# Narrow S5 kernel products, a final norm by rows, S5 scans in two parts and paired first blocks in a two-layer streaming encoder

## The chip, the cores and the metric

The kernel runs on 1 core of one Trainium2 chip. The metric is the time of one launch on the device in microseconds, as the median of several runs; less is better.

## The reference

Two layers over L = 528 positions (16 meta tokens, 512 real ones) of D = 1024 channels. Each layer projects the normalized stream once, feeds three mixers, gates, merges and projects back; a last RMSNorm ends it.

```python
for layer in range(2):
    u = _rmsnorm(h, norm_g[layer])
    (gq, gk, gv, ga, g_gate, s_in, s_gate, aq, ak, av, a_gate, m_gate) = _split_in(u @ w_in[layer])
    y_gla = (_gla_mixer(gq, gk, gv, ga, ...) * silu(g_gate)) @ w_gla_out[layer]
    y_s5  = (_s5_mixer(s_in, ...)            * silu(s_gate)) @ w_s5_out[layer]
    y_att = (_swa_mixer(aq, ak, av, ...)     * silu(a_gate)) @ w_attn_out[layer]
    gates = sigmoid(m_gate).reshape(B, L, 3, D)
    mix = gates[:, :, 0] * y_gla + gates[:, :, 1] * y_s5 + gates[:, :, 2] * y_att
    h = h + mix @ w_out[layer]
return _rmsnorm(h, final_norm_g)[:, 16:]
```

The S5 mixer runs a complex diagonal recurrence with 64 states for each group of 16 channels, then `y = gelu(y)` and `y * sigmoid(y @ w_glu)`.

## The kernel before

Everything lies channel-major: a tensor of 1024 channels is eight tiles (`kt`) of 128 partitions by 528 positions. Every large product is done in blocks of 128 output channels. A block is 24 weight tiles: weights and activations are split into a high and a low part in a rounded float type, and `WH·xh`, `WH·xl` and `WL·xh` are summed over the 8 `kt`, in two halves of 264 columns in layer 0 (48 matmuls) and mostly one of 512 in layer 1 (24).

The blocks of a layer stand in one fixed list, `BLOCKS`: ga, gk (4), gv (8), gq (4), gg (8), aq (8), ak, av; blocks of the merge of GLA (mg0 and wgla by turns, then sin, 8) between the attention steps; then `S5F` (ag, 8, and mg2 and watt by turns, 16) with the S5 steps between them; glu (8), sg (8), mg1 and ws5 by turns (16), wout (8). SyncE loads the raw weights of block n+3 into one of three slots when block n is done (`load_block`); ScalarE copies them to the high part (`hi_part`, L1143), GpSimd subtracts to the low part (`lo_part`, L641). TensorE (`project`, L756; `project_as_made`, L738, where the input comes tile by tile) writes a block into one of two PSUM slots (`RING`), and ScalarE or VectorE `take` it out. Small products go through two further PSUM slots in a fixed order (`AUX`).

S5 matrices: for each of the eight channel tiles j of layer m VectorE makes C·A^k (`cam`) and A^k·B (`mbm`), TensorE transposes them and multiplies them to the local kernel (`toep`, L805, with the skip term, L810), ScalarE evicts them, SyncE spills them to DRAM. All of this is done in layer 0, for m = 0 between gk3 and gq0 (`MATS_0`), for m = 1 between sg6 and wout4 (`MATS_1`).

S5 steps, in the stage of `S5F`: after block i = 3 TensorE computes `step_inputs(0)` (L1071). After block i = 6 + 2j it computes `step_outputs(j)` (L1084, L1086), which wait for `x_state` j, and `step_inputs(j+1)`. VectorE runs `s5_scan(ly, j+1)` after its take of the same block: products with phases from PSUM, the rotation (L1451), a copy of decays (L1943), two scans (L1946), four products and two sums to the state. VectorE's take of a watt block is one reading (L1557) and one add into the mix; an mg2 block it doesn't read.

```python
if i in S5_OUT:
    step_outputs(j)
    if j + 1 < KT:
        step_inputs(j + 1)
```

After the last wout block: squares (ScalarE), sums over channels by TensorE (L781), variance, root, reciprocal (L1499), eight scalings (L2024), 32 transposes (L1126), four copies, four stores.

Of the kernel before, what the change touches and what calls it, by code (L numbers as in the profile page):

```python
# [18 lines left out]
ALU = mybir.AluOpType  # L19
# [77 lines left out]

MATS_0 = [("gk", 3)] + [("gv", j) for j in range(1, 8)] + [("gq", 0)]
MATS_1 = [("sg", 6)] + [("ws5", j) for j in (0, 1, 2, 3, 5)] + [("wout", j) for j in (0, 2, 4)]
# [26 lines left out]
def layer_sums(ly):  # L126
# [16 lines left out]
       + layer_sums(0) + layer_sums(1))  # L143
# [17 lines left out]
def trunk(nc, x, meta_tokens, rel_bias, norm_g, w_in, gla_w_a2, gla_b_a, gla_norm_g, s5_a_re, s5_a_im,  # L161
# [3 lines left out]
    with ctx:  # L165
# [63 lines left out]
        IK = sb("s5_int", [P, DEPTH, PAIRS], I32, at=r)  # L229
        o_tmp = top[0]  # L230
# [50 lines left out]
        def mat_buffers(m, at_bb, at):  # L281
# [10 lines left out]
                toep=sb(f"s5_toep{m}", [P, QUADS, 4, 32], at=at),  # L292
                brep=sb(f"s5_brep{m}", [P, 2, QUADS, 4, 32], at=at),
                ct=[sb(f"s5_c{m}_{i}", [P, 2, QUADS, S5_GROUP], at=a) for i, a in enumerate((at_bb, at))],
                cin=sb(f"s5_c_in{m}", [P, 2, 2, 2, S5_STATE], at=at),
                dsk=sb(f"s5_skip_diag{m}", [P, P], at=at),
                eyes=sb(f"s5_skip_rows{m}", [P, 4, 32], at=at))
# [17 lines left out]
        U = sb("u_full", [P, KT, L], at=[o_ul, o_ul + WIDE])  # L315

# [40 lines left out]
        out_ready, out_stored = sem("out_ready"), [sem(f"out_stored{i}") for i in range(2)]  # L357
        fin_ready = sem("fin_ready")
        dve_step, act_step, pool_step = sem("dve_step"), sem("act_step"), sem("pool_step")

        def aux(ly, name):

            e = AUX_AT[(ly, name)]
            return e % 2, e // 2

        def aux_out(i):
            e = len(AUX) + i
            return e % 2, e // 2
# [59 lines left out]
        def aux_result(engine, ly, name):  # L428

            h, k = aux_out(name) if isinstance(name, int) else aux(ly, name)  # L430
            engine.wait_ge(aux_full[h], k + 1)
            return h

        def spilled(engine, m, j):

            engine.wait_ge(mats_spilled[j % 2], 48 * (4 * m + j // 2) + 48)
# [15 lines left out]
        def _(sp):  # L452
# [57 lines left out]
            def spill_mats(m, j):  # L510
# [10 lines left out]
                sp.dma_start(mat_part(d, "toep"), MB[m]["toep"][:].rearrange("p q t i -> p (q t i)")  # L521
                             ).then_inc(mats_spilled[j % 2], 16)
# [36 lines left out]
            for ly in range(DEPTH):  # L559
                for b in range(NB):  # L560
                    n = ly * NB + b
                    name = BLOCKS[b]
                    if name == _MERGE0[0]:

                        evacuated(sp, ly, ("ak", 0))
                        sp.dma_start(AKD[64:128, 0, :], AKD[0:64, 0, :]).then_inc(akd_loaded, 16)
                        sp.dma_start(AKD[0:64, 1, :], AKD[64:128, 1, :]).then_inc(akd_loaded, 16)
# [37 lines left out]
                    if name == ("sg", 0):  # L605
                        sp.wait_ge(yt_loaded, 256 * ly + 256)
                        sp.dma_start(H[:], HD).then_inc(h_back, 16)
                    if n + SLOTS < DEPTH * NB:
                        load_block(n + SLOTS)
            for t in range(SEQ // P):  # L610
                sp.wait_ge(out_ready, t + 1)
                sp.dma_start(out[0, P * t:P * t + P, :], XIN[:, t % 2, :]).then_inc(out_stored[t % 2], 16)
            sp.wait_ge(out_stored[0], 32)
            sp.wait_ge(out_stored[1], 32)
# [3 lines left out]
        def _(pool):  # L618
# [84 lines left out]
            for ly in range(DEPTH):  # L703
                work = phases(ly)
                for b in range(NB):
                    lo_part(ly * NB + b)
                    if b >= PHASE_FIRST:
# [4 lines left out]
        def _(pe):  # L712
# [30 lines left out]

            def project(ly, b, xh, xl):
# [27 lines left out]
            def norm_sum(k0, name, ly):  # L772

                h = aux_take(ly, name) if name else None
                if h is None:
                    h, k = aux_out(0)
                    pe.wait_ge(aux_free[h], k)
                for kt in range(KT):
                    pe.wait_ge(sq_ready, k0 + kt + 1)
                    for hf, c0, c1 in column_parts(0 if name else N_META):  # L780
# [12 lines left out]
            def step_matrices(m, j):  # L793
# [9 lines left out]
                for q in range(QUADS):  # L803
                    for ri in range(2):
                        last = pe.matmul(AX_[:, 2 * h, P * q:P * q + P],  # L805
                                         MB[m]["brep"][:, ri, q].rearrange("p a b -> p (a b)"),
                                         MB[m]["cam"][:, j % 2, ri, q, 0:4].rearrange("p a b -> p (a b)"),
                                         start=(ri == 0), stop=(ri == 1))
                        if ri == 0:
                            pe.matmul(AX_[:, 2 * h, P * q:P * q + 32],  # L810
                                      MB[m]["eyes"][:].rearrange("p a b -> p (a b)"),
                                      MB[m]["dsk"][:, 32 * q:32 * q + 32],
                                      start=False, stop=False)
                last.then_inc(aux_full[h], 1)

            def mat_turn(ly, b):
# [7 lines left out]
                if k + 1 < KT:  # L824
                    transpose_c(m, k + 1)

# [31 lines left out]
            for ly in range(DEPTH):  # L858
                norm_sum(KT * ly, ("norm", 0), ly)
                project_as_made(ly, ("ga", 0), UH, UL, ulo_ready, KT * ly)  # L860
# [10 lines left out]
                for b in BLOCKS[1:17]:  # L871
# [227 lines left out]
                project_as_made(ly, ("glu", 0), GH, GL, ylo_ready, 32 * ly + 16)  # L1099
                for j in range(1, KT):  # L1100
# [18 lines left out]

            norm_sum(KT * DEPTH, None, 0)  # L1120
            pe.wait_ge(fin_ready, KT)
            for t in range(SEQ // P):
                h, k = aux_out(1 + t)
                pe.wait_ge(aux_free[h], k)
                for kt in range(KT):
                    last = pe.transpose(AX_[:, 2 * h + kt // 4, P * (kt % 4):P * (kt % 4) + P],  # L1126
                                        H[:, kt, N_META + P * t:N_META + P * t + P], ID[:])
                last.then_inc(aux_full[h], 1)
# [3 lines left out]
        def _(act):  # L1132
# [73 lines left out]
            def matrices_out(m, j):  # L1206
# [7 lines left out]
                for p in range(STRIDE):  # L1214
                    rows = slice(32 * p, 32 * p + 32)
                    last = act.activation(
                        MB[m]["toep"][rows, :, STRIDE - 1 - p:STRIDE],
                        AX_[rows, 2 * h].rearrange("p (q t i) -> p q t i", q=QUADS, t=STRIDE)
                        [:, :, 0:p + 1], ACT.Copy)
                last.then_inc(aux_free[h], 1)  # L1220
# [32 lines left out]
            for ly in range(DEPTH + 1):  # L1253

                t0 = N_META if ly == DEPTH else 0
                for kt in range(KT):
# [7 lines left out]
                    act.activation(TA[:, kt % 2, t0:], H[:, kt, t0:], ACT.Square).then_inc(sq_ready, 1)  # L1264
                act.wait_ge(var_ready, ly + 1)
                act.activation(TD[:, 1, t0:], TD[:, 0, t0:], ACT.Sqrt).then_inc(std_ready, 1)
                if ly == DEPTH:
                    break
# [39 lines left out]
                for b in BLOCKS:  # L1308
# [4 lines left out]
                    if kind == "gv" and j % 2 == 0:  # L1313
                        log_sigmoid(j // 2)
                        if j:
                            decay_to_end(j // 2 - 1)
                    if b == ("gq", 0):
# [9 lines left out]
                    if kind == "ws5":  # L1327
                        t0 = first(ly, kind)
                        act.wait_ge(mix_ready, KT * ly + j + 1)
                        act.activation(MXH[:, j, t0:], MIX[:, j, t0:], ACT.Copy).then_inc(mhi_ready, 1)  # L1330
                    mat_turn(ly, b)
# [106 lines left out]


        @block.vector  # L1440
        def _(dve):
# [49 lines left out]
            def inverse_rms(ly, name):  # L1491

                h = aux_result(dve, ly, name)
                t0 = N_META if ly == DEPTH else 0
                dve.tensor_scalar(two(TD[:, 0], t0), halves(aslot(h), t0), 1.0 / D_MODEL, EPS, ALU.mult, ALU.add
# [3 lines left out]
                link(dve.reciprocal(TD[:, 0, t0:], TD[:, 1, t0:]))  # L1499
# [70 lines left out]
            def gla_gates(ly):  # L1570

                for hd in range(GLA_HEADS):
                    h = aux_result(dve, ly, ("gate", hd))
# [484 lines left out]
```

## Time and profile before

| | us |
|---|---|
| median of 3 runs | 1992.9 (1989.21 to 1995.55) |
| profiled execution | 1990.12 |
| its span | 1988.3 |
| TensorE busy (matmul) | 1824.9, 92% of the span |
| VectorE busy | 980.3, 49% |
| ScalarE busy | 713.2, 36% |
| GpSimd busy | 781.4, 39% |

The profile is of one execution. An engine's busy time is a mean over stages with different limits; the chain that ended last is 68% TensorE. Where TensorE waits, a view of waits names the engine and line which released it. A matmul row covers a run of like instructions; numbers in brackets are idle time before the row and who ended it.

### The profile page before, as it was taken

To read this page: it belongs to the slowest core of one execution; us is meant where nothing else is said; L and a number is where in the kernel's file an instruction comes from. 1 tells how busy PE (TensorE), PEld (TensorE's weight loads), DVE (VectorE), ACT (ScalarE), POOL (GpSimd) and SP (SyncE) were. 2 spreads that over 40 slices of the span, in tenths; PEclk is the share of its full clock that TensorE was granted. 3 is DMA by queue.
4 is the path that set the end of the run, shared out by engine and by line. 5 is a ranking of instruction groups with operands and counts; after the bars stand their busy time and mean duration, and the time that the engine had idled before them with its cause. 6 is when DMAs were issued, how large, how long until landed. Compare 5 with 4: busy or idle time off the path is not lost.

```text
span 1988.3 us, 29697 instructions
## 1 busy us (share of the span) xinstructions
PE 1824.9 (92%) x12351; PEld 1636.7 (82%) x12351; DVE 980.3 (49%) x1565; ACT 713.2 (36%) x1271; POOL 781.4 (39%) x475
## 2 busy tenths in 40 slices
PE   6977899999988999879998999999999799899996
PEld 4977898899988999879997987777788688778884
DVE  7988124422428983277663132523333589634223
ACT  3354332444542222233333453333455222223321
POOL 2544565333223333333331586653332323334440
PEclk8988899899998999989999998999999999999998
DMA  8443336222254545524443332532222645443331
GB/s 146 124 148 123 102 86 139 70 75 73 56 129 145 176 139 118 145 69 139 132 129 93 104 96 83 110 107 80 67 72 70 166 167 185 107 133 102 94 94 56
DMA packets 349758, 221.27 MB, mean 111 GB/s; under 512 B 49589, under 2 KB 338537, under 8 KB 347065
## 3 DMA queue, kind: packets, MB, share of 16 engines
q1 hardware_dynamic: 347320, 189.75, 35.8%
q10 hardware_dynamic: 2304, 29.62, 4.0%
q8 instruction: 98, 1.61, 0.3%
q14 instruction: 36, 0.29, 0.0%
HBM read 171.65 MB, written 38.50 MB: 106 GB/s over the span
## 4 chain that ended last, share of the span: by engine, by line
PE 68%; DVE 14%; POOL 5%; DMA 5%; SPq 3%; ACT 2%; issue 2%; ACTq 0%; DVEq 0%; POOLq 0%
PE ring L756 51%; DMA sb_w_raw<-in_w_in 3%; PE ring L738 3%; POOL sb_w_lo L641 2%; PE aux L992 2%; DVE sb_s_mat_prod L1451 2%; PE aux L1084 1%; PE aux L1071 1%; SPq L555 1%; PE aux L805 1%; DVE sb_s_gelu_lo L1451 1%; DVE sb_s_prod L1451 1%; PE aux L1037 1%; PE aux L1013 1%; PE aux L781 1%
## 5 line engine op out<-in xcount | busy, mean ns | idle before, releaser
L641 POOL TENSOR_TENSOR sb_w_lo<-sb_w_raw,sb_w_hi 128x1024 fp32r<-128x1024 f32 x246 | 607.2, 2470 | 1107.0 <-ACT sb_w_hi L1143 1104.7
L1143 ACT ACTIVATE sb_w_hi<-sb_w_raw 128x1024 fp32r<-128x1024 f32 x246 | 259.8, 1057 | 636.3 <-DMA sb_w_raw<-in_w_in 421.4
L756 PE MATMUL ring<-sb_u_hi,sb_w_hi 128*128 128x264 f32 (+1 forms) x2144 | 366.4, 324 | 38.8 <-DVE sb_tmp_dve L1522 28.2
L756 PEld LDWEIGHTS ring<-sb_u_hi,sb_w_hi 128*128 128x128 f32 x2144 | 311.1, 197 | 71.6 <-DVE sb_tmp_dve L1522 29.7
L756 PE MATMUL ring<-sb_u_lo,sb_w_hi 128*128 128x264 f32 (+1 forms) x2144 | 346.9, 313 | 0.0
L756 PE MATMUL ring<-sb_u_hi,sb_w_lo 128*128 128x264 f32 (+1 forms) x2144 | 338.7, 308 | 0.0
L756 PEld LDWEIGHTS ring<-sb_u_lo,sb_w_hi 128*128 128x128 f32 x2144 | 306.6, 193 | 22.3
L756 PEld LDWEIGHTS ring<-sb_u_hi,sb_w_lo 128*128 128x128 f32 x2144 | 298.0, 188 | 21.1
L1175 ACT ACTIVATE sb_tmp_act<-ring 128x528 f32<-128x528 f32 (+1 forms) x112 | 67.5, 603 | 152.1 <-PE ring L756 139.3
L1381 ACT ACTIVATE sb_att_scores<-sb_att_scores,sb_att_neg_max 128x208 f32<-128x208 f32 x128 | 58.5, 458 | 93.9 <-DVE sb_att_neg_max L1741 93.9
L756 PE MATMUL ring<-sb_y_hi,sb_w_hi 128*128 128x264 f32 (+1 forms) x504 | 87.3, 322 | 0.0
L756 PE MATMUL ring<-sb_y_lo,sb_w_hi 128*128 128x264 f32 (+1 forms) x504 | 86.3, 321 | 0.0
L756 PE MATMUL ring<-sb_y_hi,sb_w_lo 128*128 128x264 f32 (+1 forms) x504 | 86.3, 320 | 0.0
L756 PEld LDWEIGHTS ring<-sb_y_lo,sb_w_hi 128*128 128x128 f32 x504 | 73.6, 188 | 7.4
L756 PEld LDWEIGHTS ring<-sb_y_hi,sb_w_lo 128*128 128x128 f32 x504 | 73.5, 188 | 7.4
L756 PEld LDWEIGHTS ring<-sb_y_hi,sb_w_hi 128*128 128x128 f32 x504 | 73.1, 188 | 6.8
L1451 DVE TENSOR_TENSOR sb_y_lo<-sb_o_branch,sb_y_hi 128x528 fp32r<-128x528 f32 (+1 forms) x48 | 50.6, 1071 | 49.3 <-ACT sb_y_hi L1159 48.8
L1557 DVE SCALAR_TENSOR_TENSOR sb_tmp_dve<-sb_tmp_act,ring 128x528 f32<-128x528 f32 (+1 forms) x32 | 22.2, 695 | 105.4 <-PE ring L756 92.1
L1522 DVE SCALAR_TENSOR_TENSOR sb_tmp_dve<-sb_tmp_act,ring 128x528 f32<-128x528 f32 (+1 forms) x32 | 22.2, 695 | 104.1 <-ACT sb_tmp_act L1175 103.8
L1159 ACT ACTIVATE sb_y_hi<-sb_o_branch 128x528 fp32r<-128x528 f32 (+1 forms) x48 | 29.6, 633 | 76.3 <-DVE sb_o_branch L1529 55.1
L1451 DVE TENSOR_TENSOR sb_mix<-sb_mix,sb_tmp_dve 128x528 f32<-128x528 f32 (+1 forms) x32 | 55.2, 1726 | 1.1
L1557 DVE SCALAR_TENSOR_TENSOR sb_mix<-sb_tmp_act,ring 128x528 f32<-128x528 f32 (+1 forms) x16 | 11.1, 696 | 89.4 <-PE ring L756 76.3
(312 smaller groups left out, 2695.8 us busy)
## 6 DMA issues: line engine op xcount, KB each, us to landing
sb_w_raw<-in_w_in SPq DMA_DIRECT2D x166, 512.0 KB, 4.0
sb_s_loaded<-s_matrices ACTq DMA_DIRECT2D x16, 1808.0 KB, 7.3
s_matrices<-sb_s_phase SPq DMA_DIRECT2D x16, 528.0 KB, 3.2
s_matrices<-sb_s_mbt SPq DMA_DIRECT2D x16, 512.0 KB, 2.8
s_matrices<-sb_s_ca SPq DMA_DIRECT2D x16, 512.0 KB, 4.2
sb_w_raw<-in_w_gla_out SPq DMA_DIRECT2D x16, 512.0 KB, 3.9
sb_w_raw<-in_w_attn_out SPq DMA_DIRECT2D x16, 512.0 KB, 4.0
sb_w_raw<-in_s_w_glu SPq DMA_DIRECT2D x16, 512.0 KB, 4.0
```

The costliest lines, as they stand in the source:

```text
L555: sp.dma_start(BM[rows, p], bias_view(REL_ZERO - N_META - P * p - CHUNK * half, CHUNK, N_META)).then_inc(bias_in, 16)
L641: pool.tensor_tensor(WL[:, w], WR[:, w], WH[:, w].bitcast(F32), ALU.subtract).then_inc(lo_ready, 1)
L738: last = pe.matmul(RING[:, 2 * r + hf, 0:c1 - c0], w[:, n % SLOTS, kt, :], moving(b[0], xx[:, kt], c0, c1), start=(term == 0 and kt == 0), ...
L756: last = pe.matmul(RING[:, 2 * r + hf, 0:c1 - c0], w[:, n % SLOTS, kt, :], moving(b[0], xx[:, kt], c0, c1), start=(term == 0 and kt == 0), ...
L992: last = pe.matmul(AX_[:, 2 * h + a, c0:c0 + n], AQ[rows, 2 * i + h2, q0:q0 + P], AKD[rows, i // 2, keys:keys + n], start=True, stop=True)
L1143: act.activation(WH[:, w], WR[:, w], ACT.Copy).then_inc(hi_ready, 1)
L1159: act.activation(YH[:, j, t0:], src[:, t0:], ACT.Copy).then_inc(yhi_ready, 1)
L1175: act.activation(two(TA[:, t % 2], t0), ps, ACT.Tanh, scale=0.5).then_inc(done, 1)
L1381: act.activation(SC[:, u % 2, hd], SC[:, u % 2, hd], ACT.Exp, bias=NMX[:, hd:hd + 1], accum_out=SMM[:, hd:hd + 1])
L1451: return dve.tensor_tensor(o, a, b, op)
L1522: dve.scalar_tensor_tensor(two(td, t0), two(TA[:, t % 2], t0), 1.0, ps, ALU.add, ALU.mult).then_inc(free, 1)
L1557: dve.scalar_tensor_tensor(two(td, t0), two(TA[:, t % 2], t0), 1.0, ps, ALU.add, ALU.mult).then_inc(free, 1)
```

## The change

Eight edits:

- The local S5 kernel is multiplied with weights of 32 columns, eight products into four groups of PSUM partitions and one for the skip term; the copies `eyes` and `brep` and three of four evictions go. The tile is stored with six DMAs for each j in place of three.
- The matrices of m = 1 start one block earlier, their input matrices three blocks earlier, and GpSimd clears their tiles instead of VectorE.
- ScalarE adds the gates' bias instead of VectorE; in layer 1 `log_sigmoid` follows gv 0, 1, 3, 5.
- The blocks (ga0, gk0) and (glu0, glu1) are computed together, tile by tile of their input.
- The duplicate of the attention keys is copied one block earlier.
- `s5_scan` becomes a generator: its second part (scans, products, state) runs one block of `S5F` later, after that block's take.
- A small square root, so that ScalarE's table is loaded, stands ahead of the squares of each norm.
- The final norm: each finished wout tile is transposed to rows while the next block runs; squares and sums are along rows, the scale is applied to [token, channel] tiles.

```diff
-MATS_1 = [("sg", 6)] + ...
+MATS_1 = [("sg", 5)] + ...
...
+            def project_two_as_made(ly, bs, xh, xl, made, base):
+                for b, n in zip(bs, ns):
+                    r, k = ring(ly, b)
+                    if k:
+                        pe.wait_ge(slot_free[r], k)
+                    pe.wait_ge(hi_ready, n + 1)
+                    pe.wait_ge(lo_ready, n + 1)
+                for kt in range(KT):
+                    pe.wait_ge(made, base + kt + 1)
+                    for b, n in zip(bs, ns):
...
-                    for ri in range(2):
-                        last = pe.matmul(AX_[:, 2 * h, P * q:P * q + P],
-                                         MB[m]["brep"][:, ri, q].rearrange("p a b -> p (a b)"),
-                                         MB[m]["cam"][:, j % 2, ri, q, 0:4].rearrange("p a b -> p (a b)"),
...
+                for ri in range(2):
+                    for q in range(QUADS):
+                        pe.matmul(AX_[32 * q:32 * q + 32, 2 * h, 0:P], mbm[:, ri, q, 0],
+                                  cam[:, ri, q, 0:4].rearrange("p a b -> p (a b)"),
+                                  start=(ri == 0), stop=False)
+                pe.matmul(AX_[:, 2 * h, 0:32], ID[:], MB[m]["dsk"][:], start=False, stop=True
...
-                    if name == _MERGE0[0]:
+                    if name == ("av", 0):
...
                 link(dve.tensor_copy(dk[:, :, 1:STEPS],
                                      AB[:, 2, ly, qs].unsqueeze(2).broadcast_to([P, QUADS, STEPS - 1])))
+                yield
                 for ri in range(2):
                     last = dve.tensor_tensor_scan(rr[ri], MM[:, 0], rr[ri], 0.0, ALU.mult, ALU.add)
...
                         for i, f in enumerate(S5F):
                             take(ly, f)
...
                             if i in S5_OUT and S5_OUT[i] + 1 < KT:
-                                s5_scan(ly, S5_OUT[i] + 1)
+                                scan = s5_scan(ly, S5_OUT[i] + 1)
+                            next(scan, None)
...
+            def tokens_out(j):
+                evacuated(pe, DEPTH - 1, ("wout", j))
+                h = aux_take(1, ("fin", j))
+                for t in range(SEQ // P):
+                    last = pe.transpose(AX_[:, 2 * h, P * t:P * t + P],
+                                        H[:, j, N_META + P * t:N_META + P * t + P], ID[:])
...
+            def token_squares(j):
+                h = aux_result(act, 1, ("fin", j))
+                act.activation(FSQ[:, j % 2].rearrange("p t d -> p (t d)"), AX_[:, 2 * h], ACT.Square
...
+            def tokens_in(j):
+                tt(XO[:, :, P * j:P * j + P], AX_[:, 2 * h].rearrange("p (t d) -> p t d", d=P),
+                   FG[:, P * j:P * j + P].unsqueeze(1).broadcast_to([P, 4, P]), ALU.mult).then_inc(aux_free[h], 1)
+                link(dve.reduce_sum(FSS[:, :, j], FSQ[:, j % 2], AX.X))
...
+            link(act.activation(WARM[:, 0:1], ONES[:, 0:1], ACT.Sqrt))
+            token_squares(KT - 1)
...
+            for t in (2, 3):
+                act.activation(XO[:, t], XO[:, t], ACT.Copy, scale=FV[:, 0, t:t + 1]).then_inc(out_ready[1], 1)
...
+            for t in (0, 1):
+                dve.tensor_scalar(XO[:, t], XO[:, t], FV[:, 0, t:t + 1], None, ALU.mult).then_inc(out_ready[0], 1)
```

## Rows read from the trace of the kernel before

**Rows 1.** TensorE's waits over the span: total us, times, longest us.

```profile
PE aux L799 <- DVEq L1919: 28.3, 8, 8.8
PE ring L756 <- DVE sb_tmp_dve L1522: 28.2, 5, 9.2
...
PE ring L738 <- DVE sb_tmp_dve L1522: 11.3, 1, 11.3
...
PE aux L1126 <- DVE sb_residual L2024: 10.3, 1, 10.3
...
PE aux L992 <- DMA sb_att_k<-sb_att_k: 3.1, 1, 3.1
```

**Rows 2.** Windows of the S5 scans, layers 0 and 1: window, length, then busy times.

```profile
637.00:733.00 96.00, 96.00 (x808) 95.93 (x807) 87.02 (x109) 21.23 (x27) 29.49 (x12) 1.00 0.54 180
1599.00:1697.00 98.00, 97.69 (x552) 83.94 (x551) 88.81 (x114) 23.41 (x30) 29.64 (x12) 1.00 0.55 180
```

**Rows 3.** Timeline of VectorE in one turn of that stage: start us, us.

```profile
668.75 2.55 DVE L1451 TENSOR_TENSOR sb_s_prod<-aux,sb_s_loaded 128x528 f32<-128x528 f32 x4 [1.60 <-PE aux L1071]
...
674.49 2.41 DVE L1946 TENSOR_TENSOR_SCAN sb_s_rot<-sb_s_prod,sb_s_rot 128x528 f32<-128x528 f32 x2
...
679.53 1.32 DVE L1451 TENSOR_TENSOR sb_s_state<-sb_s_prod 128x524 f32<-128x524 f32 x2
680.88 0.70 DVE L1557 SCALAR_TENSOR_TENSOR sb_tmp_dve<-sb_tmp_act,ring 128x528 f32<-128x528 f32 x1
681.62 2.01 DVE L1451 TENSOR_TENSOR sb_mix<-sb_mix,sb_tmp_dve 128x528 f32<-128x528 f32 x1
```

**Rows 4.** Timeline of TensorE in the same turn.

```profile
664.85 0.61 PE L1084 MATMUL aux<-sb_s_state,sb_s_loaded 128*128 128x132 f32 x4
...
667.55 2.03 PE L1071 MATMUL aux<-sb_s_steps,sb_s_loaded 128*128 128x132 f32 x16
669.34 2.18 PE L756 MATMUL ring<-sb_y_hi,sb_w_hi 128*128 128x264 f32 x16
...
675.22 2.10 PE L756 MATMUL ring<-sb_u_hi,sb_w_hi 128*128 128x264 f32 x16
...
681.02 0.61 PE L1084 MATMUL aux<-sb_s_state,sb_s_loaded 128*128 128x132 f32 x4
```

**Rows 5.** Timeline of GpSimd in the same turn.

```profile
680.35 2.73 POOL L641 TENSOR_TENSOR sb_w_lo<-sb_w_raw,sb_w_hi 128x1024 fp32r<-128x1024 f32 x1 [7.55 <-ACT sb_w_hi L1143]
```

**Rows 6.** Timeline of VectorE and TensorE around the first scan.

```profile
615.77 4.52 DVE L1946 TENSOR_TENSOR_SCAN sb_s_rot<-sb_s_prod,sb_s_rot 128x528 f32<-128x528 f32 x2
...
625.04 3.57 PE L756 MATMUL ring<-sb_u_hi,sb_w_hi 128*128 128x264 f32 x16 [7.66 <-DVE sb_tmp_dve L1522]
```

**Rows 7.** Timeline of four engines at the start of glu, layer 0.

```profile
769.25 0.78 PE L738 MATMUL ring<-sb_s_gelu_hi,sb_w_hi 128*128 128x264 f32 x2 [3.26 <-DVE sb_s_gelu_lo L1451]
...
770.77 1.99 ACT L1143 ACTIVATE sb_w_hi<-sb_w_raw 128x1024 fp32r<-128x1024 f32 x2
...
771.89 5.36 POOL L641 TENSOR_TENSOR sb_w_lo<-sb_w_raw,sb_w_hi 128x1024 fp32r<-128x1024 f32 x2 [3.36 <-ACT sb_w_hi L1143]
...
778.46 0.71 DVE L1451 TENSOR_TENSOR sb_mix<-sb_mix,sb_tmp_dve 128x528 f32<-128x528 f32 x1
...
784.56 2.09 PE L756 MATMUL ring<-sb_s_gelu_hi,sb_w_hi 128*128 128x264 f32 x16
```

**Rows 8.** Timeline of TensorE at the first block of layer 0.

```profile
35.92 0.78 PE L738 MATMUL ring<-sb_u_hi,sb_w_hi 128*128 128x264 f32 x2 [8.76 <-DVE sb_u_lo L1451]
```

**Rows 9.** VectorE's groups by form, matrices of layer 0: busy us, mean ns.

```profile
L1917 DVE COPY sb_s_brep<-sb_s_mb 128x512 f32<-128x512 f32 x16 | 12.9, 849 | 0.0
```

**Rows 10.** Timeline of the end.

```profile
1958.29 7.59 PE L781 MATMUL aux<-sb_tmp_act,sb_ones 128*128 128x512 f32 x16
...
1979.47 6.05 SPq L612 DMA_DIRECT2D out<-sb_x_tokens  x4
...
1981.26 1.09 PE L1126 MATMUL aux<-sb_identity,sb_residual 128*128 128x128 f32 x8 [0.50 <-DVEq L2033]
```

More of the change, by code:

```diff
@@ L229, in trunk @@
         IK = sb("s5_int", [P, DEPTH, PAIRS], I32, at=r)
+        WARM = sb("act_table", [P, 8])
         o_tmp = top[0]
@@ L706, in _ @@
                     lo_part(ly * NB + b)
+                    if BLOCKS[b] == ("sg", 2) and ly == 0:
+                        aux_result(pool, 0, ("y", 6))
+                        aux_result(pool, 0, ("y", 7))
+                        produced(pool, 0, ("glu", KT - 1))
+                        for name in ("cam", "toep", "mbm"):
+                            pool.memset(MB[1][name][:], 0.0).then_inc(zeroed, 1)
                     if b >= PHASE_FIRST:
@@ L1098, in _ @@
                             step_inputs(j + 1)
-                project_as_made(ly, ("glu", 0), GH, GL, ylo_ready, 32 * ly + 16)
-                for j in range(1, KT):
+                project_two_as_made(ly, (("glu", 0), ("glu", 1)), GH, GL, ylo_ready, 32 * ly + 16)
+                for j in range(2, KT):
                     project(ly, ("glu", j), GH, GL)
@@ L1118, in _ @@
                     mat_turn(ly, ("wout", j))
[L1120 to L1128, printed above, removed]
+                    if ly == DEPTH - 1:
+                        tokens_out(j - 1)
+            tokens_out(KT - 1)
         @block.scalar
@@ L1213, in matrices_out @@
                 h = aux_result(act, m, ("toep", j))
[L1214 to L1220, printed above, removed]
+                act.activation(MB[m]["toep"][:, 3 * 32:], AX_[:, 2 * h, 0:P], ACT.Copy
+                               ).then_inc(aux_free[h], 1)
             def c_turned(m, j):
@@ L1312, in _ @@
                     block_turn(b)
[L1313 to L1317, printed above, removed]
+                    if kind == "ga":
+                        aux_read(act, -1, ("prm", 0))
+                        for hd in range(GLA_HEADS):
+                            h = aux_result(act, ly, ("gate", hd))
+                            act.activation(two(GG[:, hd]), halves(aslot(h)), ACT.Identity, bias=BA[:, ly, hd:hd + 1]
+                                           ).then_inc(aux_free[h], 1)
+                    if kind == "gv" and j in GATE_AT[ly]:
+                        hd = GATE_AT[ly].index(j)
+                        log_sigmoid(hd)
+                        if hd:
+                            decay_to_end(hd - 1)
+                    if b == (("gv", 7) if ly else ("gq", 0)):
                         decay_to_end(3)
@@ L1330, in _ @@
                         act.activation(MXH[:, j, t0:], MIX[:, j, t0:], ACT.Copy).then_inc(mhi_ready, 1)
+                    if kind == "wout" and ly == DEPTH - 1 and j:
+                        token_squares(j - 1)
                     mat_turn(ly, b)
@@ L1570, in gla_gates @@
             def gla_gates(ly):
-                for hd in range(GLA_HEADS):
-                    h = aux_result(dve, ly, ("gate", hd))
-                    dve.tensor_scalar(two(GG[:, hd]), halves(aslot(h)), BA[:, ly, hd:hd + 1], None, ALU.add
-                                      ).then_inc(aux_free[h], 1)
                 dve.wait_ge(reset_ready, 2)
```

150 lines of the change are left out of this document (82 added, 68 removed).

## The prediction

> **What bounds the kernel now.** I read the page first: TensorE is busy for 92% of the span, and the chain that ended last runs through its blocks. So an edit counts where it takes a wait out of TensorE's queue, puts one in, or changes the last part. The list of TensorE's waits [rows 1] shows where that is. The reader is to see that the waits touched here are few and long: 28.3 us in eight for the S5 matrices of layer 0, 28.2 us behind DVE's reading of blocks, 11.3 us once for the same reason, 10.3 us at the end, and twice 3.1 us for the copied keys. Then I cut stages out by time windows. During the S5 scans [rows 2] TensorE is busy for 96.00 of 96.00 us and for 97.69 of 98.00: no wait is left there to remove. DVE is busy for 87 and 89 of these. Whatever delays DVE's scan by a microsecond is paid at once if the scan's result is what TensorE asks for next. The timelines of DVE and TensorE in one turn of that stage settle whether it is [rows 3, 4].
>
> **The scans in two parts (the largest term).** One turn is 16.17 us, from the step outputs at 664.85 to the next at 681.02. In it TensorE does the outputs and inputs of a step (to 669.34), an attention-merge block (5.88 us, to 675.22) and a sigmoid block (5.80 us, to 681.02) [rows 4]. DVE starts the scan at 668.75, multiplies and rotates to 674.49, scans 2.41, multiplies 2.57, adds 1.32, and is done at 680.85: 0.17 us before TensorE starts the outputs that read it. Only after that does it read the merge block (0.70 and 2.01 us) [rows 3]. That block was ready at 675.22 and waited, but nobody waited for it.
>
> The change puts this reading in the middle of the scan. DVE is through part 1 at 674.5, now has to wait for the block's end (675.22), reads it (0.70 us, and 0.71 for the add, its time where nothing disturbs it [rows 7]), and starts part 2 at 676.8. Part 2 is 680.85 − 674.49 = 6.4 us, so x_state is ready at 683.2. TensorE wants it at 681.02: +2.2 us; in layer 1 the blocks are 0.1 us shorter each and nothing else is, so +2.4; I take +2.3 for each turn. Behind this wait on TensorE's queue stand the next inputs, from which the next scan starts: the loop is closed, the turn is lengthened each time and no later slack gives it back.
>
> Two surcharges. First, POOL's weight subtraction. Now it starts at 680.35, 5.1 us after the merge block's end, since that end frees a weight slot, and falls onto the mix add: 2.01 us instead of 0.71 [rows 3, 5]. With the new order 5.1 us after the block's end is in the middle of part 2. A scan pair that met such a subtraction took 4.52 us instead of 2.41 [rows 6]. That is +2.1; its bounds are 0 (it falls beside) and its whole length, 2.4 where nothing stretches it. I take 2.2. Second, TensorE's clock. After a wait of 7.66 us a third of a block took 3.57 us instead of 2.10 [rows 6], so the granted clock was at its lower level (1.2 GHz) for that stretch; other waits of 3 to 5 us in this trace are followed in part by slow products and in part not. A wait of 4.5 us each turn is between: 0 to 2.4 us, taken as 1.2. Together 2.3 + 2.2 + 1.2 = 5.7 us a turn. There are six such turns in each layer (scans 2 to 7), 12 in all: **+68 us** (12 × 2.3 = 28 at the least, 12 × 6.9 = 83 at the most).
>
> At the stage's start the same edit gains: the wait of 7.66 us [rows 6] (9.2 in layer 1) came from a first scan that held up DVE's readings, and these now come between. But scans 0 and 1 themselves come later, by one reading each and more, and the outputs wait for them. By the chain worked forward I get −4 to +3 in both layers together; taken 0.
>
> The Trainium skill (SBUF — State Buffer, section "SBUF: two separate sides") has DVE and GpSimd take an exclusive lock on a shared port pair for a whole instruction when a DVE operation reads two inputs from SBUF. The trace agrees: 4.52 against 2.41 us. By that rule alone part 2, all of whose inputs lie in SBUF, pays up to one subtraction of 2.4 us, and part 1's first products, which read PSUM, pay none; the sum would be 12 × 0.2 = 2 us higher.
>
> **First blocks in pairs.** In glu TensorE starts at 769.25, while ACT makes hi of the second block (with the third's) from 770.77, and POOL its lo after that: two in 5.36 us from 771.89, the first done at about 774.3 [rows 7]. The pair waits for it. It then computes two blocks, cold at first, as the rows of this place show (0.78 us for the first two products against 0.24 apiece once warm): 5.3 us of cold work and 8.6 warm, 14 us in all, to 788.2, against 784.56 before [rows 7]. +3.7, and +4.0 in layer 1: **+7.7** (5 to 9). In ga/gk both weights are there early. Single products arrive with u_lo from 35.92 [rows 8], the pair fills the waits between them and hides the gates' latency: −1.8 in layer 0 and −2.5 in layer 1, of which the Sqrt table's load ahead of the squares takes 1.4 back. **−3** (0 to −5).
>
> **S5 matrices, layer 0.** DVE makes eight sets. The two copies per set go (16 in 12.9 us), of which I count 7 us on DVE's path, as the rest of the stage idles after a set; so does most of the narrow diagonal (1 us), and DVE's own short waits for the toeplitz products shrink with them: −11 to −13 [rows 9]. The new products are nine instead of sixteen plus eight, so TensorE loses under a microsecond of work. TensorE waits 28.3 us there [rows 1], which is the most that could go. The extra issues (SP, three per set) lie in a queue with nothing urgent there. **−12** (−6 to −28).
>
> **S5 matrices, layer 1.** TensorE's one wait of 11.3 us [rows 1] ends with DVE's reading of a block behind the input matrices, three memsets and the first set. Memsets go to POOL, the input matrices two blocks earlier, the set one earlier, each in a gap of a block. Wait and the slow products behind it go, and some 2 us come back from what stands next in line, the second set: **−9** (−4 to −13).
>
> **Keys' copy.** One block earlier; each of two waits of 3.1 us then ends with the value copies, 1.9 us sooner, and in part the slow stretch behind it: **−4.5** (−3.7 to −7.7).
>
> **Gates on ACT.** Four additions of 0.77 us leave DVE in each layer, where it idles, and go to ACT, where it does too: 0. If ACT were late, gq0's reading would show it.
>
> **Final norm by rows.** Before, from the last block's end at 1958.06 to the end at 1988.3 are 30.2 us: sums 7.59 us, a reciprocal, eight scalings, 32 transposes, four stores [rows 10]. The new one puts six sets of four transposes into the wout stage. Eight take 1.09 us [rows 10], so a set 0.5 and all +3.0. After the last block: reading 0.9, transposes 0.6, table load and squares 2.0, sum and small operations 2.6, first scaling 1.1: 7.2 us to the first tile. The four stores were issued within 6.05 us [rows 10], and as the same bytes now go out together I take 6.6 with the landing, and 0.6 for semaphores. 3.0 + 7.2 + 6.6 + 0.6 = 17.4 instead of 30.2: **−12.8** (−11 to −14).
>
> **Sum.** −12 − 4.5 − 9 − 3 − 12.8 = −41.3; +7.7 + 68 = +75.7; in all +34. The profiled execution took 1990.1 us (span 1988.3), 0.14% under the median of the runs, 1992.9. 1990.1 + 34 = **2024 us**.
>
> **Rivals.**
> - A: the clock holds through the short waits. 4.5 us a turn: 54 instead of 68, **2010 us**. For it: no row shows a wait of just this length at a steady rhythm.
> - B: the clock falls fully after each: 6.9 us a turn, 83, **2039 us**.
> - C, the other side: POOL's subtraction misses part 2 and the clock holds. Then 12 × 2.3 = 28, and the start gains its 4: 1990.1 − 41.3 + 7.7 + 28 − 4 = **1980 us**, faster. It decides from (41.3 − 7.7) / 12 = 2.8 us a turn. For it: the subtraction starts from a DMA's landing, which can be later when the turn is longer. Against: 5.1 us after the block's end held in the turns I looked at.
> - D: the split costs nothing, because part 1 waits for something else, or the reading hides in a gap I don't see. Then 1990.1 − 41.3 + 7.7 = 1956, **1953 us** with the start's gain. Against: DVE's chain has 0.17 us of slack [rows 3, 4].
>
> **Chances and range.** Forecast 0.38, A 0.22, B 0.12, C 0.18, D 0.10. The range runs from 1978 (C within it at its edge) to 2042: D and the edges left out are 0.2. Times of single runs differ by 0.3%, so that much tells nothing from no change: faster by more 0.25, within 0.06, slower 0.69.
>
> **What would show it.** In the turn of the scans: a TensorE wait before the step outputs released by DVE's s_state, 12 times, of 4.5 us; the turn at 20 to 22 us; the mix add at 0.71 us and a scan or product pair stretched. Before glu a wait of 8 us in place of 3.3. No wait of 11 us before the first ws5 block; fewer matrix waits than 28.3 us. At the end 14 us behind the last block. The prediction is wrong if the turn stays near 16.2 us, or if the first waits of the stage don't vanish.

## The result, and the profile after

The changed kernel takes 2052.9 us (median of 4 runs, 2051.31 to 2056.71) against 1991.7 us before (4 runs): a ratio of 1.031, 95% interval 1.029 to 1.033. That is +61 us, where +34 was forecast. The direction and the main place are right; the size is not, and 2052.9 lies above the range of 1978 to 2042.

TensorE's waits over the span after (total us, times, longest us), against [rows 1]:

```profile
PE aux L1125 <- DVE sb_s_state L1504: 71.5, 16, 5.8
PE ring L776 <- DVE sb_tmp_dve L1609: 26.6, 2, 13.6
PE aux L825 <- ACT sb_s_mbt L1245: 20.9, 11, 3.5
PE ring L795 <- DVE sb_tmp_dve L1574: 20.5, 5, 7.4
PE aux L835 <- DVEq L1962: 20.4, 5, 8.7
```

Three things are new. The step outputs (L1125) wait for the state 16 times, once per step and layer, for 71.5 us. The pairs (L776) wait twice for a reading of VectorE at L1609, which is that of a watt block: 13 us each. And TensorE waits 11 times for ScalarE's eviction of the matrices (4.5 us in 4 before). The waits of 28.3 us for the matrices of [rows 1] are 20.4, that of 11.3 us is gone from the list, and so is that of the last transposes.

One turn of the scans, TensorE after (start us, us), against [rows 4]:

```profile
674.99 1.25 PE L1125 MATMUL aux<-sb_s_state,sb_s_loaded 128*128 128x132 f32 x4 [4.34 <-DVE sb_s_state L1504]
...
680.43 2.10 PE L1112 MATMUL aux<-sb_s_steps,sb_s_loaded 128*128 128x132 f32 x16
682.28 2.20 PE L795 MATMUL ring<-sb_y_hi,sb_w_hi 128*128 128x264 f32 x16
...
688.18 2.10 PE L795 MATMUL ring<-sb_u_hi,sb_w_hi 128*128 128x264 f32 x16
...
698.47 1.25 PE L1125 MATMUL aux<-sb_s_state,sb_s_loaded 128*128 128x132 f32 x4 [4.33 <-DVE sb_s_state L1504]
```

VectorE in the same turn, against [rows 3]:

```profile
685.94 0.43 DVE L1987 COPY sb_s_prod<-sb_s_a 128x524 f32<-128x524 f32 x1
...
688.44 0.70 DVE L1609 SCALAR_TENSOR_TENSOR sb_tmp_dve<-sb_tmp_act,ring 128x528 f32<-128x528 f32 x1 [2.07 <-issue]
689.18 0.71 DVE L1504 TENSOR_TENSOR sb_mix<-sb_mix,sb_tmp_dve 128x528 f32<-128x528 f32 x1
689.92 2.41 DVE L1991 TENSOR_TENSOR_SCAN sb_s_rot<-sb_s_prod,sb_s_rot 128x528 f32<-128x528 f32 x2
692.36 4.71 DVE L1504 TENSOR_TENSOR sb_s_prod<-sb_s_loaded,sb_s_rot 128x528 f32<-128x528 f32 x4
697.10 1.32 DVE L1504 TENSOR_TENSOR sb_s_state<-sb_s_prod 128x524 f32<-128x524 f32 x2
```

GpSimd in it, against [rows 5]:

```profile
694.06 2.44 POOL L651 TENSOR_TENSOR sb_w_lo<-sb_w_raw,sb_w_hi 128x1024 fp32r<-128x1024 f32 x1 [9.35 <-ACT sb_w_hi L1177]
```

Of the kernel before, [rows 3] leave out the four products of this turn:

```profile
676.93 2.57 DVE L1451 TENSOR_TENSOR sb_s_prod<-sb_s_loaded,sb_s_rot 128x528 f32<-128x528 f32 x4
```

The turn is 698.47 − 674.99 = 23.5 us instead of 16.17. VectorE has finished part 1 at 686.4, stands 2.07 us until the watt block is done, reads it, and only then scans. The four products take 4.71 us instead of 2.57, and the subtraction at 694.06 falls into them (experiment 7 tests this), 5.9 us after the block's end at 688.2. TensorE waits 4.33 us. Then the outputs take 680.43 − 674.99 = 5.44 us instead of 667.55 − 664.85 = 2.70 [rows 4]. The windows of this turn say why (window, length, busy times of the five engines; the third figure from the end is TensorE's granted clock as a share of full speed):

```profile
674.90:680.40 5.50, 5.42 (x24) 5.42 (x25) 0.03 (x1) 0.00 (x0) 0.00 (x0) 0.50 0.02 3
680.40:694.00 13.60, 13.60 (x114) 13.53 (x112) 9.91 (x15) 2.62 (x3) 2.41 (x1) 0.99 0.52 176
```

The clock is at 0.50, its lower level, through all of the outputs, and back for the blocks. The stall is paid a second time. This turn is one of the dearest: in others the clock came back before the outputs had ended. In the next one the first four matmuls took 1.25 us again, but the third four only 0.68:

```profile
724.95 0.68 PE L1125 MATMUL aux<-sb_s_state,sb_s_loaded 128*128 128x132 f32 x4
```

Over both layers the trace has 14 turns, of 23.0 us in the mean against 16.0 before.

The start of glu, four engines after, against [rows 7]:

```profile
791.13 4.36 ACT L1482 ACTIVATE sb_s_gelu_hi<-sb_s_in 128x528 fp32r<-128x528 f32 x8
791.87 10.49 DVE L1504 TENSOR_TENSOR sb_s_gelu_lo<-sb_s_in,sb_s_gelu_hi 128x528 fp32r<-128x528 f32 x8 [11.61 <-ACT sb_s_gelu_hi L1482]
...
796.52 5.28 POOL L651 TENSOR_TENSOR sb_w_lo<-sb_w_raw,sb_w_hi 128x1024 fp32r<-128x1024 f32 x2 [3.35 <-ACT sb_w_hi L1177]
...
802.28 0.69 DVE L1609 SCALAR_TENSOR_TENSOR sb_tmp_dve<-sb_tmp_act,ring 128x528 f32<-128x528 f32 x1
803.29 0.78 PE L776 MATMUL ring<-sb_s_gelu_hi,sb_w_hi 128*128 128x264 f32 x2 [12.97 <-DVE sb_tmp_dve L1609]
```

The second block's low weights are there at about 799. The pair starts at 803.29, after VectorE's reading of the last watt block at 802.28, which stands behind the eight low parts of gelu on VectorE's queue: that block holds the PSUM slot that glu1 needs.

The end after, against [rows 10]:

```profile
2037.35 0.60 PE L864 MATMUL aux<-sb_identity,sb_residual 128*128 128x128 f32 x4
...
2043.02 1.42 DVE L2088 TENSOR_SCALAR sb_out_tokens<-sb_out_tokens,sb_out_var 128x1024 f32<-128x1024 f32 x2
2043.02 2.19 ACT L1490 ACTIVATE sb_out_tokens<-sb_out_tokens,sb_out_var 128x1024 f32<-128x1024 f32 x2 [0.24 <-DVE sb_out_var L2085]
2043.80 2.89 SPq L623 DMA_DIRECT2D out<-sb_out_tokens  x4
```

From the last block's end (2037.1) to the span's end (2050.8) are 13.7 us instead of 30.2.

### The profile page after: what moved, and what is told of

The parts are those of the page before. It is cut to its first block and busy times, and to the rows that moved or that the text cites. A ratio compares the mean times of both kernels' runs of the same rounds, so it can differ in the third digit from the quotient of the medians.

```text
span 2050.8 us, 29472 instructions
## 1 busy us (share of the span) xinstructions
PE 1819.2 (89%) x12239; PEld 1629.6 (79%) x12239; DVE 967.6 (47%) x1527; ACT 693.9 (34%) x1236; POOL 782.7 (38%) x478
## 5 line engine op out<-in xcount | busy, mean ns | idle before, releaser
L795 PE MATMUL ring<-sb_u_hi,sb_w_lo 128*128 128x264 f32 (+1 forms) x2112 | 334.5, 309 | 0.0
L1125 PE MATMUL aux<-sb_s_state,sb_s_loaded 128*128 128x132 f32 x256 | 67.7, 415 | 71.5 <-DVE sb_s_state L1504 71.5
L1125 PEld LDWEIGHTS aux<-sb_s_state,sb_s_loaded 128*128 128x128 f32 x256 | 59.3, 316 | 76.7 <-DVE sb_s_state L1504 76.7
L1609 DVE SCALAR_TENSOR_TENSOR sb_tmp_dve<-sb_tmp_act,ring 128x528 f32<-128x528 f32 (+1 forms) x32 | 22.2, 695 | 144.7 <-PE ring L795 85.5
L1504 DVE TENSOR_TENSOR sb_s_prod<-aux,sb_s_loaded 128x528 f32<-128x528 f32 x64 | 40.8, 699 | 77.8 <-PE aux L1112 77.7
L1504 DVE TENSOR_TENSOR sb_y_lo<-sb_o_branch,sb_y_hi 128x528 fp32r<-128x528 f32 (+1 forms) x48 | 46.3, 979 | 49.8 <-ACT sb_y_hi L1193 49.2
L1504 DVE TENSOR_TENSOR sb_s_prod<-sb_s_loaded,sb_s_rot 128x528 f32<-128x528 f32 x64 | 68.8, 1136 | 0.6
```

Source lines behind the costliest of these rows:

```text
L795: last = pe.matmul(RING[:, 2 * r + hf, 0:c1 - c0], w[:, n % SLOTS, kt, :], moving(b[0], xx[:, kt], c0, c1), start=(term == 0 and kt == 0), ...
L1125: pe.matmul(dst, cam[:, ri, q], XX[:, ri, q, :], start=(ri == 0), stop=False)
L1504: return dve.tensor_tensor(o, a, b, op)
L1609: dve.scalar_tensor_tensor(two(td, t0), two(TA[:, t % 2], t0), 1.0, ps, ALU.add, ALU.mult).then_inc(free, 1)
```

## The experiments

Before is shared by the kernels run together, and lay between 1989.4 and 1990.7 us in these. Each median is of 4 to 6 runs; a single run strays by up to 11 us from it, most by less than 6.

**1. The scans in one part again, in the changed kernel.**

```diff
-                            next(scan, None)
+                            for _ in scan:
+                                pass
```

> The changed kernel with the scans in one part again, everything else as changed. Theory (the split is the whole loss: seven turns in each layer, 7.0 us longer each, less some 9 us that it gains on TensorE's first long waits of the stage): 2053 - 98 + 9 = 1964 us, turns back at 16.2 us. Rival (part of the long turns comes from something else that was changed, the matrices' new layout or the pairs): the turns stay above 17 us and the time is over 1985 us.

Measured: 1959.3 us, ratio to before 0.986 (0.982 to 0.989). The split alone costs 2052.9 − 1959.3 = 94 us. In the trace 12 of the 14 turns are at 15.8 to 16.3 us again; one of the other two (19.0 us) has a wait for the state of 2.7 us. The first waits of the stage return:

```profile
PE ring L795 <- DVE sb_tmp_dve L1574: 34.0, 6, 9.4
PE ring L776 <- DVE sb_tmp_dve L1609: 27.4, 2, 13.9
```

**2. glu0 alone again, in the changed kernel.**

```diff
-                project_two_as_made(ly, (("glu", 0), ("glu", 1)), GH, GL, ylo_ready, 32 * ly + 16)
-                for j in range(2, KT):
+                project_as_made(ly, ("glu", 0), GH, GL, ylo_ready, 32 * ly + 16)
+                for j in range(1, KT):
```

> The changed kernel with glu0 alone again, tile by tile, and glu1 after it. Theory (the pair has to wait for two PSUM slots, and the second is held by the last watt block until VectorE has made all eight low parts): the wait of 13 us ahead of glu goes, 15 us less in all, 2038 us. Rival (the pair waits for the second block's low weights, as predicted): 7.7 us less, 2045 us.

Measured: 2037.7 us, ratio 1.026 (1.023 to 1.029): the pair costs 15 us, twice the prediction's 7.7.

**3. Both back.** The edits of 1 and 2 together.

> The changed kernel with the scans in one part and glu0 alone, both again as before. Theory (the two add up): 2053 - 89 - 15 = 1949 us. Rival (they overlap, since the start of glu is set by the same chain): above 1957 us.

Measured: 1945.8 us, ratio 0.979 (0.977 to 0.981). The two add up (94 + 15 = 109; 2052.9 − 1945.8 = 107), and all the other edits together are worth some 44 us.

**4. The split alone, in the kernel before.** `yield` in `s5_scan` and `next(scan, None)` as in the change, nothing else.

> The kernel before with the scans in two parts and nothing else. Theory: +98 for the turns, -9 for the first waits: 1992 + 89 = 2081 us, in every turn a wait of 4.3 to 4.8 us ahead of the step outputs and outputs at half rate. Rival (the split costs 5.7 us in 12 turns as predicted, the rest of the loss is elsewhere): 2060 us.

Measured: 2083.6 us, ratio 1.047 (1.044 to 1.051): +94 us, the same price in the other kernel. Its trace shows what that is made of: the 14 turns together are 100 us longer than before, and the first outputs of layer 0 come 6 us earlier (at 626.37 instead of 632.32 us).

```profile
PE aux L1084 <- DVE sb_s_state L1451: 73.5, 16, 5.8
```

**5. TensorE kept busy through the wait.** In the changed kernel:

```diff
                 def step_outputs(j):
 
+                    h = aux_take(ly, ("y", j))
+                    mbt = mat_part(MSB[:, j % 2], "mbt").rearrange("p (r q m) -> p r q m", r=2, q=QUADS)
+                    for r in range(4):
+                        for q in range(QUADS):
+                            pe.matmul(AX_[:, 2 * h + q // 2, STEPS * (q % 2):STEPS * (q % 2) + STEPS],
+                                      mbt[:, r % 2, q, :], Z4[:, j, q, :], start=True, stop=True)
                     pe.wait_ge(x_state, 8 * ly + j + 1)
```

> The changed kernel; ahead of the wait for each state TensorE multiplies 16 tiles (some 3.5 us) into the PSUM slot that the step outputs then overwrite, so that it is busy in most of the 4.4 us. Theory (the outputs run at half rate because TensorE stood still before them): outputs in 2.7 us again instead of 5.4, 14 to 16 times, so 2053 - 36 = 2017 us although the work is more. Rival (the outputs are slow for another reason, as their operands): no change or some us more, 2053 to 2060.

Measured: 2017.8 us, ratio 1.015 (1.013 to 1.018): 35 us less, with more work. TensorE in one turn, and the clock of its outputs:

```profile
666.70 3.76 PE L1122 MATMUL aux<-sb_s_steps,sb_s_loaded 128*128 128x132 f32 x32
671.23 0.72 PE L1130 MATMUL aux<-sb_s_state,sb_s_loaded 128*128 128x132 f32 x4 [0.77 <-DVE sb_s_state L1509]
...
674.03 2.03 PE L1112 MATMUL aux<-sb_s_steps,sb_s_loaded 128*128 128x132 f32 x16
```

```profile
671.20:674.00 2.80, 2.77 (x24) 2.77 (x25) 0.00 (x0) 0.00 (x0) 0.00 (x0) 1.00 0.03 6
```

The outputs take 2.80 us at a clock of 1.00 instead of 5.44 at 0.50. The half rate was a consequence of the idle time. 35 us for 16 outputs are 2.2 us each, a little less than the 2.6 of this turn, since the clock came back inside some of them. One of the 16 was still slow here (4.4 us, behind a wait of 2.2 in layer 1).

**6. The last watt block read before the low parts.** In the changed kernel:

```diff
-                            if i == S5_SPLIT:
+                            if i == S5_SPLIT + 1:
                                 for t in range(KT):
                                     dve.wait_ge(yhi_ready, 32 * ly + 16 + t + 1)
```

> The changed kernel; VectorE reads the last watt block before it makes the eight low parts, not after. Theory (the pair waits for the PSUM slot of that block): the wait ahead of glu is then set by the second block's low weights, some 4 us less in each layer, 2045 us. Rival (it waits for the low parts or weights anyway): 2053.

Measured: 2045.8 us, ratio 1.029 (1.027 to 1.031), 7 us less. TensorE now waits for what the prediction had named:

```profile
PE ring L776 <- POOL sb_w_lo L651: 19.5, 2, 10.1
```

**7. No subtraction on GpSimd in the turns.** In the changed kernel, for the blocks of mg2 and watt. This kernel leaves their low weights out and puts a copy of the raw ones in their place; it shows a time, and is no version to use.

```diff
             def lo_part(n):
                 pool.wait_ge(hi_ready, n + 1)
                 w = n % SLOTS
+                if BLOCKS[n % NB] in S5F[8:]:
+                    return
+                pool.wait_ge(lo_ready, n)
...
                 act.activation(WH[:, w], WR[:, w], ACT.Copy).then_inc(hi_ready, 1)
+                if BLOCKS[n % NB] in S5F[8:]:
+                    act.wait_ge(hi_ready, n + 1)
+                    act.wait_ge(lo_ready, n)
+                    act.activation(WL[:, w], WR[:, w], ACT.Copy).then_inc(lo_ready, 1)
```

> The changed kernel with a part of the computation changed: for the blocks of mg2 and watt GpSimd makes no low weights; ScalarE writes a copy of the raw ones in their place. Theory (GpSimd's subtraction holds up VectorE's second part by 2.2 us a turn): the wait ahead of the outputs falls from 4.4 to 2.3 us, and the time by 14 times 2.2 us, 2022 us, or down to 1984 if TensorE's clock holds through the shorter wait. Rival (the products of part 2 are slow for another reason): waits stay above 4 us, 2050.

Measured: 2002.1 us, ratio 1.006 (1.004 to 1.008): 51 us less. TensorE and then VectorE in two turns:

```profile
661.38 0.72 PE L1128 MATMUL aux<-sb_s_state,sb_s_loaded 128*128 128x132 f32 x4 [2.20 <-DVE sb_s_state L1511]
...
680.02 1.25 PE L1128 MATMUL aux<-sb_s_state,sb_s_loaded 128*128 128x132 f32 x4 [2.19 <-DVE sb_s_state L1511]
```

```profile
673.61 2.41 DVE L1998 TENSOR_TENSOR_SCAN sb_s_rot<-sb_s_prod,sb_s_rot 128x528 f32<-128x528 f32 x2
676.05 2.57 DVE L1511 TENSOR_TENSOR sb_s_prod<-sb_s_loaded,sb_s_rot 128x528 f32<-128x528 f32 x4
```

The products are back at 2.57 us and the wait is 2.2 us: the structural part of the prediction to a tenth. TensorE's waits for the state are 40.4 us over the span instead of 71.5. After the same wait of 2.2 us the outputs are fast in one turn (0.72) and at half rate in the next (1.25). Of the 12 outputs that followed a wait of 2.2 to 2.4 us, three took 2.8 us and nine 4.2 to 4.5, so the clock's share is between the two cases of the expectation.

**8. Only the first scan of each layer in two parts, glu0 alone.**

```diff
                             next(scan, None)
+                            if i > S5_IN:
+                                for _ in scan:
+                                    pass
```

> As the kernel with scans whole and glu0 alone (1945.8 us), but the first scan of each layer in two parts. Theory (the split's gain on TensorE's waits of 7.7 and 9.2 us comes from the first scan alone, whose outputs come three blocks later and have slack): 9 us less, 1937. Rival (the first outputs then wait instead): 1946 or more.

Measured: 1938.9 us, ratio 0.975 (0.973 to 0.978). Against the kernel of experiment 3 that is 7 us less; the two intervals just overlap (that of experiment 3 begins at 0.977), so the difference isn't clear of noise by itself. The waits agree with it: those for VectorE's readings fall from 34.7 us in experiment 3 to 18.8, and the first outputs now wait, as the rival had it, but for less:

```profile
PE ring L795 <- DVE sb_tmp_dve L1574: 18.8, 6, 7.7
PE aux L1125 <- DVE sb_s_state L1504: 10.0, 3, 5.0
```

This kernel is the base of the next ones.

**9 to 12. One edit back at a time, from the kernel of 8.** ga alone before gk0; the gates' bias on VectorE; the matrices of m = 1 after sg6 with their input matrices; the keys' copy one block later.

> The kernel with only the first scan split and glu0 alone (1938.9 us), and ga computed alone before gk0 as in the kernel before. Theory (the pair hides the gates' latency and computes gk0 warm, which the traces put at 4.7 us in layer 0 and 5.7 in layer 1): 10 us more, 1949. Rival (my prediction's 3 us): 1942.

> The kernel with only the first scan split and glu0 alone (1938.9 us), and VectorE adds the gates' bias again. Theory (both engines idle there): no change, 1939 within 0.3%. Rival (VectorE's line to the first matrices is shorter by the four additions): 3 to 4 us more, 1942.

> The kernel with only the first scan split and glu0 alone (1938.9 us), and the matrices of m = 1 start after sg6 again with their input matrices (GpSimd still clears the tiles). Theory (the earlier start took 6 us from one wait but clearing on GpSimd alone takes 4 of them): 2 to 4 us more, 1942. Rival (the earlier start is worth the predicted 9 us): 1946 or more.

> The kernel with only the first scan split and glu0 alone (1938.9 us), and the keys copied after av again. Theory (two waits of 1.9 us and some of the slow stretch behind each): 4.5 us more, 1943. Rival (the copy is hidden either way): 1939.

Measured: 1938.7, 1946.7, 1939.0 and 1941.3 us (ratios 0.976, 0.980, 0.975, 0.976, each about ±0.003). The pair of ga and the early start of m = 1 show no gain that this can tell from none, the keys' 2 us are within the noise, and the gates' bias, costed at nothing, is worth 8 us. Its interval (0.977 to 0.982) and that of its base just overlap too, but the traces put the 8 us in one place: the first products of the attention in layer 0 start at 362.29 us instead of 353.93. VectorE in the kernel with the bias on it, and then in its base:

```profile
50.12 1.66 DVE L1620 TENSOR_SCALAR sb_gla_decay<-aux,sb_params 128x528 f32<-128x528 f32 x2 [6.00 <-PE aux L909]
...
54.14 0.21 DVE L1498 TENSOR_TENSOR sb_s_small<-sb_s_small 128x64 f32<-128x64 f32 x1
```

```profile
44.08 0.22 DVE L1504 TENSOR_TENSOR sb_s_small<-sb_s_small 128x64 f32<-128x64 f32 x1
```

The additions are 3 us, but they stand first in VectorE's queue and wait there for TensorE's gates. The preparation of the matrices behind them, which needs no gate, starts at 54.14 instead of 44.08.

**13. The wide products again, from the kernel of 8.** The local S5 kernel's matmuls, copies, evictions and stores as before.

> The kernel with only the first scan split and glu0 alone (1938.9 us), and the local S5 kernel computed with the wide products, the copies and four evictions of the kernel before. Theory (in layer 0 VectorE's line loses the copies, some 8 to 10 us; in m = 1 the products' time comes back as a wait for ScalarE): 9 us more, 1948. Rival (my terms: 12 for m = 0 and a part of the 9 for m = 1): 1953 or more. Second rival (the whole gain of that stage came with the gates and the pair): 1940.

Measured: 1945.9 us, ratio 0.977 (0.975 to 0.979). The narrow products are worth 7 us by the medians, with intervals that overlap a little. In the traces 6 us of it are there when the attention of layer 0 starts (359.97 us instead of 353.93), behind the stage of m = 0, and the stage of m = 1 adds none that can be told from noise.

**14. C transposed first.** From the kernel of 8, in TensorE's and ScalarE's order and in the order of the PSUM slots:

```diff
-                if k:
-                    step_matrices(m, k - 1)
-                else:
+                if not k:
                     transpose_c(m, 0)
                 if k + 1 < KT:
                     transpose_c(m, k + 1)
+                if k:
+                    step_matrices(m, k - 1)
```

> The kernel with only the first scan split and glu0 alone (1938.9 us), and for each set TensorE transposes C of the next set ahead of B's transposes and the local kernel, and ScalarE evicts them in that order. Theory (TensorE's 11 waits of 20.6 us in all are for the PSUM slot that ScalarE has yet to empty; with C first the slot is free): 10 to 15 us less, 1926. Rival (the wait moves to the local kernel's products, which then need the slot of C): no change, 1939.

Measured: 1941.4 us, ratio 0.974 (0.972 to 0.977): no change. The wait went with the order of the slots, from the C transposes to the products:

```profile
PE aux L842 <- ACT sb_s_c L1258: 17.7, 7, 3.7
```

**15. ScalarE evicts first.** From the kernel of 8. ScalarE in the kernel of experiment 3 shows the reason: it evicts at 882.79, right behind the high part of the mix, for which it stood idle 3.05 us.

```profile
882.25 0.64 ACT L1373 ACTIVATE sb_mix_hi<-sb_mix 128x528 fp32r<-128x528 f32 x1 [3.05 <-DVE sb_mix L1504]
882.79 1.01 ACT L1245 ACTIVATE sb_s_mbt<-aux 128x1024 f32<-128x1024 f32 x1
```

```diff
                     if kind == "ws5":
+                        mat_turn(ly, b)
                         t0 = first(ly, kind)
                         act.wait_ge(mix_ready, KT * ly + j + 1)
                         act.activation(MXH[:, j, t0:], MIX[:, j, t0:], ACT.Copy).then_inc(mhi_ready, 1)
...
-                    mat_turn(ly, b)
+                    if kind != "ws5":
+                        mat_turn(ly, b)
```

> The kernel with only the first scan split and glu0 alone (1938.9 us), and in the ws5 stage ScalarE evicts the matrices ahead of the high part of the mix instead of behind it. Theory (the five waits of some 2 us each are ScalarE standing behind VectorE's add into the mix): they fall to about 0.4 us and the time by 8 to 10 us, 1930. Rival (TensorE then waits for the mix or VectorE's next set): no change in the time, 1939.

Measured: 1924.3 us, ratio 0.967 (0.965 to 0.969), 15 us less. TensorE's waits for ScalarE in this stage, in its base and here:

```profile
PE aux L825 <- ACT sb_s_mbt L1245: 12.7, 6, 3.4
PE aux L825 <- ACT sb_s_mbt L1245: 2.1, 6, 0.4
```

That is 10.6 us of the 15. Behind such a wait TensorE was slow as well: a third of a block took 3.41 us after a wait of 2.35 in the base, and 2.18 after one of 0.29 here.

It is the fastest version run: 66 us under the kernel before, 129 under the changed one.

## Why the prediction was wrong, by its steps

**The turn of the scans: mechanism right, size short.** The wait of VectorE for the watt block, the 2.2 us of structure (2.2 in experiment 7) and the subtraction's 2.2 (a wait of 4.3 against 2.2) were measured as forecast. The Trainium skill (SBUF — State Buffer, section "SBUF: two separate sides") says that the port pair that VectorE and GpSimd share is an exclusive lock, held for a whole instruction by whichever of the two started first, where VectorE's instruction reads two inputs from SBUF. The trace agrees: 4.71 us for products that take 2.57 without the subtraction.

Two terms of the sum were too small. The first is the clock: "0 to 2.4 us, taken as 1.2". It was 5.44 − 2.70 = 2.7 us in the turn shown, and filling the wait gave 35 us back, 2.2 for each of 16 outputs (experiment 5). I had taken a middle between rows at either level. But of the 16 waits in the changed kernel the 15 of 4.2 us and more all had slow matmuls behind them, so a clock that held never occurred there. The turn shown is 23.5 us, against the 21.9 of the forecast and the 23.1 of rival B; in the mean a turn is 7.0 us longer instead of 5.7.

The second is the count: 12 turns, and 0 for the first ones, which I had let cancel against the gain at the start. Scan 1 pays like the others (turns of 23.7 and 24.1 us), so there are 14 turns of 7.0 us, 98 us, and the start gives back some 6 (experiment 4's trace). 68 forecast, 94 measured (experiments 1 and 4).

**The pair in glu: the wrong wait.** "The pair waits for it", the second block's low weights. It waits for two PSUM slots, and the second is freed by a reading that stands behind 10.5 us of low parts on VectorE's queue. I listed what the new instruction waits for in weights and not in slots. 7.7 forecast, 15 measured. Experiment 6 separates them: with the slot freed early the wait is on the low weights, as forecast, and 7 us shorter.

**The other edits: the sum nearly right, from wrong terms.** −41 forecast, −44 measured (experiment 3). That the two are so near is chance, as the terms show. The final norm was −12.8. By the traces it is 30.2 − 13.7 = 16.5 us, less seven sets of transposes (not six) of 0.5 us, so −13; no run had it by itself. The gates' bias was 0 and is −8 (experiment 10): I looked at whether VectorE was idle, and not at what stood behind the additions in its queue. The narrow products and what goes with them in layer 0 were −12; the products alone are −7 (experiment 13). The prediction's "nine instead of sixteen plus eight" sets nine instructions against 24 rows of the trace, which shows each of these instructions as two; it is nine instead of twelve, and no term hung on it. The early start of m = 1 with the clearing on GpSimd was −9; the early start alone is 0 (experiment 11), and the clearing wasn't tried. In the changed kernel's trace its long wait shrinks from 11.3 to 5.3 us, while TensorE's waits for ScalarE in that stage grow from 4.5 to 11.3: TensorE arrives earlier at an eviction that stands behind the mix. Experiments 14 and 15 show that this eviction sets the pace there: another order of the transposes and their evictions gave no change (1941.4 against 1938.9 us), and the eviction ahead of the mix gained 15 us. The pair of ga was −3 and the keys −4.5; neither is told from 0, nor quite from the forecast.

**What stays open.** The gates' bias (8), the narrow products (7), the keys (2 at most) and the final norm by the traces (13) make 30 of the 44 us. Clearing the tiles on GpSimd, the small square roots and the order of the logarithms in layer 1 weren't tried by themselves. The traces say where to look: from the start of layer 1's norm to its first attention products the kernel before takes 283.4 us and that of experiment 3 takes 273.2, 10 us less. With the pair of ga, the gates' bias or the keys' copy taken back (experiments 9, 10, 12) that stretch is 276.2, 272.6 and 277.7 us, against 273.3 in their base, so part of the 10 lies with none of them or is noise. That edits which shorten one line of work are worth more together than one at a time is possible too, and not shown.

## What to carry to other kernels

Where the bounding engine is 100% busy and another engine hands over its result 0.2 us early, anything put into that engine's line is paid, even if it only fills a wait of somebody else. A wait that came back in every turn cost itself here (4.5 us) and 2.2 us of half rate on TensorE behind it. For an instruction that takes two resources at once, list the holder of each, PSUM slots too, and find that holder's release in its own queue. An operation's price can be what stands behind it in the queue and not its duration: four additions of 0.77 us cost 8 us, and an eviction moved ahead of a wait gained 15.

## What the runs showed of the hardware

After a wait of 4.3 us the granted clock was 0.50 for the whole 5.4 us of outputs, and with 3.8 us of matmuls put into the wait it was 1.00. Ahead of the step outputs of the changed kernel 15 of 15 waits of 4.2 to 5.8 us were followed by slow matmuls, in some turns only for the first half of the outputs. After a wait of 2.2 us both levels occurred in consecutive turns (0.72 and 1.25 us for the same four matmuls), so a wait of that length doesn't decide it. Beside an instruction of GpSimd with two inputs from SBUF (2.44 us) four products of VectorE took 4.71 us instead of 2.57; with its work on ScalarE instead there was no such stretch.
